# Down tiles of an 8-expert layer issued by ScalarE on a DMA queue of its own

## What is computed

```python
D_FF = 7 * D_MODEL // 2          # 3584
N_EXPERTS_2 = 8

def _moe_swiglu_layer(x, norm_g, w_router, w_gate, w_up, w_down):
    xt = _rms_norm(x, norm_g).reshape(-1, d)
    logits = xt.astype(jnp.float32) @ w_router.astype(jnp.float32)
    top_vals, top_idx = lax.top_k(logits, TOP_K)
    gates = jax.nn.softmax(top_vals, axis=-1)
    ...
    def expert_block(args):
        xb, e = args
        return (jax.nn.silu(xb @ w_gate[e]) * (xb @ w_up[e])) @ w_down[e]
    ...
    out = jax.ops.segment_sum(ys.astype(jnp.float32) * slot_w[:, None], slot_tok, num_segments=n_tok)
    return x + out.reshape(b, s, d).astype(x.dtype)
```

## Time and profile before

| | |
|---|---|
| median of 3 executions | 2015.64 us (2014.34 to 2017.02) |
| profiled execution | 2013.11 us |
| its span | 2011.3 us |
| granted TensorE clock, mean | 0.958 |
| PE busy (matmul) | 1828.7 us, 91% |
| DVE busy | 751.5 us, 37% |
| ACT busy | 304.7 us, 15% |
| weight traffic of queue q1 | 644.68 MB |

### The profile page before, as it was taken

How to read it: one execution, slowest core, us unless ns; L and a number is a source line. 1 busy time by engine, 2 the same in 40 slices (tenths; PEclk the granted TensorE clock), 3 DMA queues, 4 the chain that set the end, 5 groups by cost and what they waited for, 6 DMA issues and landing times.

```text
span 2011.3 us, 29199 instructions
## 1 busy us (share of the span) xinstructions
PE 1828.7 (91%) x12660; PEld 932.8 (46%) x12660; DVE 751.5 (37%) x1443; ACT 304.7 (15%) x557; POOL 59.3 (3%) x39
## 2 busy tenths in 40 slices
PE   9998987677666799999999999999999999989997
PEld 6787642222222266577777663343334333323332
DVE  4486543333333458335668642110110021112213
ACT  3244221111111126201010030000000000000000
POOL 0017000000000000000000000000000000000000
PEclk9999997877787999999999999999999999999999
DMA  7202499999999961353535358999999999999997
GB/s 268 107 7 87 183 409 431 431 430 430 431 430 430 426 262 43 141 241 126 199 140 205 127 210 338 429 431 431 431 430 430 430 432 429 429 432 429 430 430 305
DMA packets 52260, 646.61 MB, mean 321 GB/s; under 512 B 8352, under 2 KB 10912, under 8 KB 13344
## 3 DMA queue, kind: packets, MB, share of 16 engines
q1 hardware_dynamic: 52128, 644.68, 76.4%
HBM read 643.61 MB, written 1.05 MB: 321 GB/s over the span
## 4 chain that ended last, share of the span: by engine, by line
PE 80%; DMA 11%; issue 3%; DVE 3%; ACT 1%; SPq 0%; DVEq 0%; ACTq 0%
PE low L1020 39%; PE high L1020 38%; DMA slot<-in_moe_w_up 9%; DMA slot<-in_moe_w_down 2%; PE low L1810 1%; DVE hact L2922 1%; PE high L1310 0%; ACT slot L2401 0%; DVE x_sb L2929 0%; PE low L1034 0%; DMA x_sb<-in_x 0%; DVE sg L2922 0%; PE high L1242 0%; DVE sca L2922 0%; PE low L1046 0%
## 5 line engine op out<-in xcount | busy, mean ns | idle before, releaser
L1020 PE MATMUL high<-slot,ffn_tail 128*64 128x512 f32 (+2 forms) x1232 | 242.9, 601 | 2.1 <-DMA slot<-in_moe_w_down 2.1
L1020 PE MATMUL low<-slot,hT 128*64 128x512 f32 (+2 forms) x896 | 223.9, 605 | 4.0 <-DMA slot<-in_moe_w_up 2.1
L1020 PE MATMUL high<-slot,xgT 128*32 128x512 f32 (+1 forms) x1168 | 185.8, 662 | 37.0 <-issue 19.1
L1020 PE MATMUL low<-hT,slot 128*128 128x256 f32 (+1 forms) x1008 | 209.9, 369 | 0.5 <-DVE hT L2922 0.5
L1020 PE MATMUL low<-slot,xgT 128*32 128x512 f32 (+2 forms) x864 | 177.2, 669 | 31.2 <-issue 18.0
L1020 PEld LDWEIGHTS low<-hT,slot 128*128 128x128 f32 x1008 | 183.9, 190 | 27.3 <-issue 3.3
L1020 PEld LDWEIGHTS high<-slot,ffn_tail 128*64 128x64 f32 (+2 forms) x1232 | 75.9, 130 | 161.3 <-issue 157.3
L1020 PEld LDWEIGHTS low<-slot,xgT 128*32 128x32 f32 (+2 forms) x864 | 56.6, 139 | 137.9 <-issue 131.2
L1020 PEld LDWEIGHTS high<-slot,xgT 128*32 128x32 f32 (+1 forms) x1168 | 52.5, 123 | 144.2 <-issue 134.9
L1020 PEld LDWEIGHTS low<-slot,hT 128*64 128x64 f32 (+2 forms) x896 | 69.1, 138 | 107.2 <-issue 101.6
L1020 PE MATMUL high<-slot,hT 128*128 128x512 f32 (+1 forms) x224 | 98.5, 587 | 1.9 <-ACT hT L2401 1.4
(11 more groups left out here) (499 smaller groups left out, 2050.2 us busy)
## 6 DMA issues: line engine op xcount, KB each, us to landing
slot<-in_moe_w_up SPq DMA_DIRECT2D x88, 2048.0 KB, 24.9
slot<-in_moe_w_down SPq DMA_DIRECT2D x87, 2048.0 KB, 24.6
slot<-in_moe_w_gate SPq DMA_DIRECT2D x68, 2048.0 KB, 20.5
tables<-in_moe_w_gate SPq DMA_DIRECT2D x19, 2048.0 KB, 26.7
slot<-in_dffn_w_down SPq DMA_DIRECT2D x7, 2048.0 KB, 7.4
slot<-in_dffn_w_gate SPq DMA_DIRECT2D x7, 2048.0 KB, 7.4
slot<-in_dffn_w_up SPq DMA_DIRECT2D x7, 2048.0 KB, 11.9
slot<-in_w_in_tiles SPq DMA_DIRECT2D x6, 2048.0 KB, 8.6
```

Of the source, the lines that this page charges most:

```text
L1020: return nc.tensor.matmul(o, l, r, start=start, stop=stop)
```

## The change

SyncE no longer issues the down tiles of units 3 to 55. ScalarE issues them, in its own instruction stream and so on its own DMA queue. The down tile of unit n + 1 is issued by ScalarE in its turn for unit n, ahead of unit n's silu, behind a wait for `down_read`, which says that the down product of unit n - 2 has read the place. SyncE keeps gate and up with the waits they had. The wait for `lined_up` moves from ahead of the loop to each first read of an expert's number, on both engines. ScalarE's other branch (`dense`, taken when the experts have too many tokens for the rooms above) is written out in full for this layer with the same loads.

```diff
--- before.py
+++ after.py
@@ -813,6 +813,20 @@
             eng.wait_ge(slot_in[i], 16 * n)
             return slot[i]
 
+        def mixed_load(eng, expert_of, n, j):
+
+            k, c = mix2.seq[n]
+            s = load_place(n, j)
+            src = (a["moe_w_gate_2"], a["moe_w_up_2"], a["moe_w_down_2"])[j]
+            if k == LAST:
+                src = src[FIXED * NFC + c]
+            else:
+                if k not in expert_of:
+                    eng.wait_ge(lined_up, 1)
+                    expert_of[k] = eng.value_load(lineup[0:1, k:k + 1], min_val=0, max_val=N_E2 - 1)
+                src = src[bass.ds(expert_of[k] * NFC + c, 1), :, :].rearrange("o p n -> (o p) n")
+            eng.dma_start(slot[s][:, :, :].rearrange("p a b -> p (a b)"), src).then_inc(slot_in[s], 16)
+
         win = lambda i: a["w_in_tiles"][i]
         by_tile_ = lambda *names: [f"{n}{t}" for n in names for t in range(TT)]
         ROOTS = by_tile_("ln1") + ["gla", "kk"] + by_tile_("gn", "ln2", "halves") + ["lat", "heads"] + \
@@ -985,27 +999,14 @@
 
             def chunk(n, j):
 
-                k, c = mix2.seq[n]
-                s = load_place(n, j)
-                src = (g2_, u2_, d2_)[j]
-                if k == LAST:
-                    src = src[FIXED * NFC + c]
-                else:
-                    if k not in expert_of:
-                        expert_of[k] = sp.value_load(lineup[0:1, k:k + 1], min_val=0, max_val=N_E2 - 1)
-                    src = src[bass.ds(expert_of[k] * NFC + c, 1), :, :].rearrange("o p n -> (o p) n")
-                sp.dma_start(flat_slot(s), src).then_inc(slot_in[s], 16)
-
-            sp.wait_ge(lined_up, 1)
+                mixed_load(sp, expert_of, n, j)
+
             for n in range(3, UNITS + 1):
                 if n < UNITS:
                     sp.wait_ge(gate_read, N_E1 + n - 2)
                     chunk(n, 0)
                     sp.wait_ge(gu_read, N_E1 + NFC + n - 2)
                     chunk(n, 1)
-                if n > 3:
-                    sp.wait_ge(down_read, N_E1 + NFC + n - 3)
-                    chunk(n - 1, 2)
             parts = out[0].rearrange("(t p) (c d) -> p t c d", p=P, c=2)
             for j in range(4):
                 t, c = j // 2, j % 2
@@ -2568,7 +2569,19 @@
                     b = V.bank(phase + h)
                     f(sg[:, h % 2, :], b[:, 0:T], ACT.Silu).then_inc(done, 1)
 
+            def down_load(n, expert_of):
+
+                if 1 <= n < UNITS - 2:
+                    act.wait_ge(down_read, N_E1 + NFC + n)
+                    mixed_load(act, expert_of, n + 2, 2)
+
             def dense(x):
+                if x is moe2:
+                    expert_of = {}
+                    for n in range(UNITS):
+                        gates(0, 4 * n, 4, x.hid_filled, x.hid_emptied, x.dense_silu)
+                        down_load(n, expert_of)
+                    return
                 with act.Fori(0, x.count * x.nfc) as i:
                     gates(0, 4 * i, 4, x.hid_filled, x.hid_emptied, x.dense_silu)
 
@@ -2798,7 +2811,9 @@
 
             def packed(x):
                 m, ring = mix2, mix2.ring
+                expert_of = {}
                 for n, (k, c) in enumerate(m.seq):
+                    down_load(n - 1, expert_of)
                     rows_ = slice(0, ROOM[k])
                     if m.wide(k):
                         act.wait_ge(m.gate_filled, m.gates_before(n) + 1)
```

## The result

| | before | with the change |
|---|---|---|
| median | 2015.56 us (2014.34 to 2017.02, 6 executions) | 2023.28 us (2021.15 to 2024.83, 6 executions) |
| ratio, 95% interval | | 1.0041 (1.0031 to 1.0051) |
| profiled execution, span | 2013.11, 2011.3 us | 2024.83, 2022.9 us |

The account below looks back on a forecast made before the run. DMA engines were taken to bound the layer, TensorE trailing closely. Issuing 0, wait 0, end of transfers 0 and tail 6.3 us gave 2021.9 us from 2015.64; likeliest case 2019.4 to 2024.4, whole range 2013 to 2031 us.

Parts of the forecast that it names:

- The bound: 8-expert layer, 1216 to 1991 us: DMA engines bound it at 429 GB/s, TensorE trails closely, SyncE waits for places.
- Issuing and the new wait at nothing: On ScalarE: 53 issues of 0.33 us and its wait for `down_read` ahead of each silu cost 0 us.
- The equal share: Both loading queues share the DMA engines equally; a down tile lands after about 9.8 us of transfer, delaying overtaken tiles 4.89 us each.
- Rival A: Both engines' issues in the layer are served in order of arrival, so time stays at 2015.6 us; chance 0.20.
- rivals B and C: DMA rate over the layer's 775 us: rises, 2004.2 us, chance 0.14; or falls, 2029.7 us at 1% loss, chance 0.12.
- None of this lengthens the layer by itself: Waits near units 8 and 41, up 41 coming 5 to 10 us later: DMA engines stay busy, last transfer's end unchanged.
- The tail, +6.3 us: Last unit: down 54, and down 55 in part, overtake up 55; middle of +3.8 and +8.7 us.
- the upper bound of +8.7: Last unit: down 54 and down 55 both overtake up 55, +9.8 - 1.1 us, if TensorE is not later than before.
- the landing times: Down tiles of the layer, on the second queue, land 10 to 15 us after issue.
- the first wait: Near unit 8, about 1300 us: TensorE waits some 2 us for up 8, more if its line holds two down tiles.
- the longer wait at unit 41: TensorE waits longer than 7.85 us for up 41, which comes 5 to 10 us later.
- The sign of the tail: At unit 55 TensorE's last wait is for an up or gate tile, no longer the last down tile; about 22 us remain.

Follow-up runs that it names:

- e1: Kernel before plus only the change's wait: ScalarE waits for `down_read` ahead of silus of units 2 to 54, issuing nothing; 2012.12 us against 2013.17, ratio 0.9995.
- e10: Changed kernel, but ScalarE issues all 159 tiles from unit 3 on in the old order, SyncE none; 2014.66 us against 2013.33, ratio 1.0007.
- e8: Changed kernel, but ScalarE issues only down tiles of units 3 to 45, SyncE those of 46 to 55 in old order; 2022.94 us against 2014.14, ratio 1.0039.
- e9: Changed kernel, but ScalarE issues only the down tiles of units 36 to 45, SyncE the rest in old order; 2022.48 us against 2014.14, ratio 1.0039.
- e3: Changed kernel, but ScalarE issues only the down tiles of units 3 to 10, SyncE the other 45 in old order; 2013.31 us against 2013.17, ratio 0.9998.
- e5: Changed kernel, but ScalarE issues only the last ten down tiles, of units 46 to 55; 2023.97 us against 2012.22, ratio 1.0051.

## Why the prediction was right, and where it was not

**The bound.** Right. The DMA engines are full at 430 GB/s, and the places, not the issues, hold SyncE.

**Issuing and the new wait at nothing.** Right, shown apart in e1 and e10.

**The equal share.** Right: from 1210 to 1800 us every tile of the second queue took 13.4 to 15.5 us to land, whatever lay in the first. Rival A (order and time stay) is refuted by that, rivals B and C (the rate rises or falls) by 430 GB/s with both queues at work.

**"None of this lengthens the layer by itself ... the line is 5 to 8 tiles long and shrinks by one or two at most."** This step failed. The delay of up 41 was put at 5 to 10 us and waved through, since the DMA engines would stay busy. It was 13.6 us in the trace (and gave 10.8 and 11.9 us of lag in e8 and e9), and it did lengthen the layer. The prediction itself had read TensorE's waits and could have seen it: between its wait at 1782.35 us and its wait at 1987.98 us TensorE waits for no tile. There it is as much a bound as the DMA engines, so a lag that it takes on at unit 41 stays until unit 55, where it can give back 3.9 us, and no more. At units 7 and 8 a lag of 7.3 us is free, since 7.85 us of waiting lie ahead (e3). And the transfers don't stay full either: 2.8 us of them were lost from 1900 to 1930 us.

**The tail, +6.3 us.** The term has about the size of the result and isn't what happened in the change: there TensorE waits for no tile at unit 55. The tail comes into its own where TensorE is less late (e5: +10.3 us, the upper bound of +8.7 being within its interval of 7.4 to 12.9). In the full change the lag at unit 41 takes its place: 13.6 - 3.9 - 1.0 us. Both are a few overtaking tiles of 4.89 us less what the end gives back, but one doesn't follow from the other. The direction came from the right cause, tiles that are overtaken, but at the wrong place; that the size came out within 1.4 us is in good part luck. (The upper end of its range, 2024.4 us, should be 2015.64 + 8.7 = 2024.3.)

**The signs to look for.** The second queue, the landing times, the first wait (at unit 7, one unit earlier than said, where the prediction had worked out unit 8; up 8, put at 1302.2 us with one tile overtaking it, was taken at 1310.32 us, less 2.83 1307.5, so that two had) and the longer wait at unit 41 came as described. The sign of the tail, a last wait for an up tile of unit 55, did not.

## What to carry to other kernels

Where the DMA engines are full, as here, a second queue adds nothing to the rate; it only changes which tile lands first, and it favours the queue with the shorter line. Before a load is moved to another queue, ask which tile of the old line is wanted first, how many new ones can overtake it, and how much waiting its reader has ahead in which the delay can vanish. For that last question look for the last stretch in which the reader never waits: a delay in front of it goes to the end, a delay in front of a wait that is longer than it costs nothing.

## What the runs showed of the hardware

A 3.45 us wait of TensorE at unit 7 put it to the lower clock. From the stretches before the wait and behind it (granted clock third from the end):

```profile
core 0: us, PE busy (x) PEld busy (x) DVE busy (x) ACT busy (x) POOL busy (x), PEclk, DMA share, GB/s
1285.00:1292.00 7.00, 7.00 (x36) 2.39 (x35) 1.12 (x2) 0.59 (x1) 0.00 (x0) 1.00 1.00 431
1296.00:1299.00 3.00, 3.00 (x8) 0.87 (x8) 0.00 (x0) 0.00 (x0) 0.00 (x0) 0.50 0.98 421
```

1.00 is 2.4 GHz, 0.50 is 1.2 GHz, and the product behind took 6.39 in place of 3.60 us: the clock added 2.8 us to a wait of 3.45. The wait of 0.74 us at unit 8 left the next product at 3.65 us. The length of a wait alone doesn't tell what the clock does: behind 2.12 us before the product took 4.48 us, behind 3.12 us with the change 2.78 us, behind 3.13 us at the same place of e8 5.34 us. The last two, first with the change and then in e8:

```profile
1780.60:1783.30 2.70, 2.70 (x24) 0.77 (x25) 0.00 (x0) 0.00 (x0) 0.00 (x0) 1.00 1.03 443
```

```profile
1782.00:1787.00 5.00, 4.76 (x24) 1.12 (x24) 0.00 (x0) 0.00 (x0) 0.00 (x0) 0.50 0.99 423
```

That two queues share the DMA engines equally was an assumption before. It held closely: alone in its queue, a tile of 2.097 MB took 13.4 to 15.5 us from 1210 to 1800 us, while SyncE's tiles took anything from 12.6 to 36.4 us. The very last down tile, issued at 1993.85 us, had the DMA engines to itself from 1996.3 us on, when up 55 and down 54 had landed, and took 9.2 us: one transfer of 4.89 us and some 4 us around it.
